# Two reorderings in a fused two-block transformer kernel: state products inside a projection block, and attention quarters of one wide and one narrow query tile

## What is computed

```python
n = rms_norm(h, attn_norm[i])
z = n @ w_in[i]
gq, gk, gv, g_low, g_r, c_q, c_kv, k_r = split_cols(z, IN_SPLITS)
...
def step(state, inp):                      # linear attention, chunks of 64 tokens
    qi, ki, vi, gi = inp
    b = jnp.cumsum(gi, axis=2)
    b_last = b[:, :, -1:, :]
    o_inter = jnp.einsum('bhtk,bhkv->bhtv', qi * jnp.exp(b), state)
    ...
    k_dec = ki * jnp.exp(b_last - b)
    state = state * jnp.exp(b_last[:, :, 0, :, None]) + jnp.einsum('bhsk,bhsv->bhkv', k_dec, vi)
    return state, o_inter + o_intra
...
for blk in range(S // Q_BLOCK):            # latent attention, query tiles of 128 tokens
    qs, qe = blk * Q_BLOCK, (blk + 1) * Q_BLOCK
    qb, kb, vb = q[:, qs:qe], k[:, :qe], v[:, :qe]
    logits = jnp.einsum('bqhd,bkhd->bhqk', qb, kb).astype(jnp.float32) * scale
    ...
    probs = jax.nn.softmax(logits, axis=-1).astype(vb.dtype)
    outs.append(jnp.einsum('bhqk,bkhd->bqhd', probs, vb))
...
h = h + jnp.concatenate([o_g, o_m], axis=-1) @ w_out[i]
```

## Time and profile before

| | |
|---|---|
| median of three runs | 2522.47 us (2522.36 to 2523.17) |
| the profiled execution | 2522.89 us, its span 2521.2 us |
| PE busy | 2457.1 us (97%) |
| DVE busy | 1695.4 us (67%) |
| ACT busy | 1061.8 us (42%) |
| linear attention behind the last projection block | about 226 to 297 us of the span |
| latent attention's 64 units | about 356 to 516 us of the span |

### The profile page before, as it was taken

The page is one execution under the profiler, slowest core; times in us unless marked ns, Lnnn a source line. Parts: engine busy times, 40 slices in busy tenths (PEclk is TensorE's granted clock), DMA queues, the critical chain, the costliest instruction groups (busy, mean ns, idle before and its releaser), DMA issues.

```text
span 2521.2 us, 29558 instructions
## 1 busy us (share of the span) xinstructions
PE 2457.1 (97%) x11406; PEld 1948.0 (77%) x11406; DVE 1695.4 (67%) x2062; ACT 1061.8 (42%) x1500; POOL 125.6 (5%) x215
## 2 busy tenths in 40 slices
PE   8999888999999999999999999999999999999998
PEld 6877755578888888888788777778778888888885
DVE  5237777644877768698873555345578877686888
ACT  5225576634433333333542323343355433334336
POOL 1001000000000010000001000000001000000001
PEclk9998899999999999999999999999999999999999
DMA  5110000033432372600134121124435433616103
GB/s 220 45 42 22 1 1 1 18 133 125 146 114 100 114 278 77 234 1 17 51 108 137 42 67 67 67 100 150 150 126 196 147 114 120 217 51 217 50 1 134
DMA packets 76179, 252.13 MB, mean 100 GB/s; under 512 B 6288, under 2 KB 6320, under 8 KB 76016
## 3 DMA queue, kind: packets, MB, share of 16 engines
q1 hardware_dynamic: 43792, 131.08, 16.0%
q0 software_dynamic: 32256, 119.27, 12.6%
HBM read 186.76 MB, written 62.91 MB: 99 GB/s over the span
## 4 chain that ended last, share of the span: by engine, by line
PE 75%; DVE 10%; issue 3%; ACT 3%; DVEq 0%; ACTq 0%
PE ps L2593 23%; PE ps L2933 20%; PE ps L2971 18%; PE ps L3099 6%; DVE opQ_lo L2037 1%; PE ps L3027 1%; PE ps L3045 1%; DVE opQ_lo L2034 1%; PE ps L2866 1%; DVE spot L2079 1%; DVE ql_raw L2074 1%; PE ps L2896 1%; PE ps L2710 1%; PE ps L2817 1%; PE ps L3036 1%
## 5 line engine op out<-in xcount | busy, mean ns | idle before, releaser
L2971 PE MATMUL ps<-opQ_hi 128*128 128x512 f32 x896 | 350.3, 391 | 2.8 <-DVE opQ_lo L2037 2.8
L2971 PE MATMUL ps<-opQ_hi,opQ_lo 128*128 128x512 f32 x896 | 348.7, 389 | 0.0
L2971 PE MATMUL ps<-opQ_lo,opQ_hi 128*128 128x512 f32 x896 | 348.6, 389 | 0.0
L2593 PE MATMUL ps<-opP_hi,w_hi 128*128 128x512 f32 x640 | 199.6, 393 | 2.3 <-ACT Z L1094 1.1
L2971 PEld LDWEIGHTS ps<-opQ_hi 128*128 128x128 f32 x896 | 168.2, 188 | 42.1 <-DVE opQ_lo L2037 7.2
L2593 PE MATMUL ps<-opP_lo,w_hi 128*128 128x512 f32 x640 | 197.6, 390 | 0.0
L2593 PE MATMUL ps<-opP_hi,w_lo 128*128 128x512 f32 x640 | 197.5, 390 | 0.0
L2971 PEld LDWEIGHTS ps<-opQ_hi,opQ_lo 128*128 128x128 f32 x896 | 168.2, 188 | 35.2
L2971 PEld LDWEIGHTS ps<-opQ_lo,opQ_hi 128*128 128x128 f32 x896 | 168.2, 188 | 34.6 <-issue 0.2
L1214 ACT ACTIVATE opQ_hi<-spot 128x1024 fp32r<-128x1024 f32 x80 | 84.9, 1061 | 235.7 <-PE ps L2971 196.7
L823 ACT ACTIVATE w_hi<-w_stage 128x1024 fp32r<-128x1024 f32 x104 | 109.3, 1051 | 171.8 <-PE ps L2593 148.2
(11 more groups left out here) (425 smaller groups left out, 4809.3 us busy)
## 6 DMA issues: line engine op xcount, KB each, us to landing
w_stage<-in_w_stream SPq DMA_DIRECT2D x104, 512.0 KB, 3.7
h_spill<-T POOLq DMA_DIRECT2D x56, 512.0 KB, 4.9
pair_raw<-in_w_stream SPq DMA_DIRECT2D x26, 1024.0 KB, 5.8
spot<-in_w_stream SPq DMA_DIRECT2D x24, 1024.0 KB, 7.3
spot<-h_spill POOLq DMA_DIRECT2D x24, 1024.0 KB, 9.3
qh_raw<-in_w_stream SPq DMA_DIRECT2D x8, 1024.0 KB, 11.3
ql_raw<-h_spill POOLq DMA_DIRECT2D x8, 1024.0 KB, 8.1
g_spill<-T POOLq DMA_DIRECT2D x16, 512.0 KB, 2.9
```

Source lines behind the costliest of these rows:

```text
L2593: mm = pe.matmul(ps[:, psum + half, :], weight, operand[:, k, half * HALF:(half + 1) * HALF], start=(begin and x == 0 and weight is wh and ...
L2971: mm = pe.matmul(ps[:, down_bank(sc, f) + m, :], weight, operand, start=(g == 0 and kt == 0 and weight is wh and operand is hi), stop=(g = ...
```

## The change

The linear attention's first state products are put between the two halves of the last projection block, the states' folding on DVE is moved ahead with them, and ACT's list is reordered. In the latent attention the quarters become (7, 0), (6, 1), (5, 2), (4, 3), and inside a quarter the wide and the narrow tile alternate. All of the diff is shown but for two short stretches.

```diff
@@ -40,7 +40,7 @@
...
-QBLOCKS = [(pr, qt, par) for pr in range(MH // 2) for qt in range(WIN) for par in range(2)]
+QBLOCKS = [(pr, qt, par) for pr in range(MH // 2) for q in range(4) for par in range(2) for qt in (7 - q, q)]
@@ -310,8 +310,8 @@
             "lexp", "qx", "lk", "lmm", "lcp", "out", "oraw", "sq", "nst", "rn", "sig", "gated", "normed", "fin")}
-        g["dot"], g["wide"] = g["logit"], g["soft"]
-        DOT, WIDE = 2, 1
+        g["dot"], g["wide"], g["upper"] = g["logit"], g["soft"], g["lin"]
+        DOT, WIDE, UPPER = 2, 1, 2
         m = {n: sem("lat_" + n) for n in ("stat", "r", "lat", "sq", "ln")}
@@ -411,7 +411,7 @@
         LEVEL_ORDER = (0, 1, 3, 8, 2, 4, 5, 6, 7, 9, 10, 11)
-        EARLY_LEVELS = 5
+        EARLY_LEVELS = 6
@@ -635,7 +635,7 @@
             pool.memset(QE[0][:, :, :, :, :], 0.0).then_inc(g["zero"], 1)
-            pool.wait_ge(mm_done, B_WOUT)
+            pool.wait_ge(g["upper"], UPPER + 1)
             for pr in range(2):
@@ -960,7 +960,6 @@
             level(8)
-            act.wait_ge(mm_done, B_WOUT)
             level(2)
@@ -988,13 +987,13 @@
             blocks_out(0)
+            level(4)
+            blocks_out(2)
+            diagonal(1, range(WIN)).then_inc(g["diag"], 1)
+            blocks_out(1)
             act.activation(EB[:, :, :], Bc[:, :, :], ACT.Exp, scale=1.0 / 16).then_inc(g["exps"], 1)
...
                 level(n)
-                if n == 4:
-                    blocks_out(2)
-                    diagonal(1, range(WIN)).then_inc(g["diag"], 1)
-                    blocks_out(1)
                 if n == 9:
@@ -1091,8 +1090,9 @@
                 act.wait_ge(mha["pv"], 2 * i + 2)
-                act.activation(Z[:, 8 + i // 2, (i % 2) * HALF:(i % 2 + 1) * HALF], ps[:, 6 + i % 2, :], ACT.Copy)\
-                   .then_inc(mha["o"], 1)
+                tiles = Z[:, 8 + i // 2, :].rearrange("p (x c) -> p x c", c=2 * P)
+                act.activation(tiles[:, 1:3, :] if i % 2 else tiles[:, 0:4:3, :],
+                               ps[:, 6 + i % 2, :].rearrange("p (x c) -> p x c", c=2 * P), ACT.Copy).then_inc(mha["o"], 1)
@@ -1110,12 +1110,12 @@
                     act.wait_ge(mha["pv"], u // 4)
-                act.activation(PT[:, par, 0:n, (qt % 2) * P:(qt % 2 + 1) * P], ps[:, 4, 0:n * P].rearrange("p (k t) -> p k t", t=P),
+                act.activation(PT[:, par, 0:n, (qt // 4) * P:(qt // 4 + 1) * P], ps[:, 4, 0:n * P].rearrange("p (k t) -> p k t", t=P),
                                ACT.Copy).then_inc(mha["ea"], 1)
...
                     act.wait_ge(mha["tb"], upper_groups(u + 1))
-                    act.activation(PT[:, par, 4:4 + n, (qt % 2) * P:(qt % 2 + 1) * P],
+                    act.activation(PT[:, par, 4:4 + n, P:2 * P],
                                    ps[:, 5, 0:n * P].rearrange("p (k t) -> p k t", t=P), ACT.Copy).then_inc(mha["eb"], 1)
@@ -1740,8 +1740,6 @@
             v.tensor_tensor(QK[:, :, :], q_t, k_t, ALU.mult).then_inc(g["qk"], 1)
-            win_step(B_WIN + 15, None, 15, 1, False)
@@ -1749,10 +1747,10 @@
-            def states(pr):
+            def states(pr, steps=range(NCH - 1)):
                 v.wait_ge(g["upd"], pr + 1)
-                for c in range(NCH - 1):
+                for c in steps:
@@ -1776,23 +1774,26 @@
+            v.wait_ge(g["upper"], UPPER + 1)
             exponents(2)
-            factors(2)
-            exponents(4)
             v.wait_ge(g["consts"], 16)
...
                 v.memset(ST8[:, pr, 0, :], 0.0).then_inc(g["states"], 1)
-            states(0)
+            states(0, range(0, 6))
+            win_step(B_WIN + 15, None, 15, 1, False)
+            states(0, range(6, NCH - 1))
+            factors(2)
+            exponents(4)
             for n in range(3, len(GLA_STEPS)):
...
                 if n == 3:
-                    inter_queries(0)
+                    states(1)
                 if GLA_STEPS[n - 1][1] >= 2:
...
                 if n == 4:
-                    states(1)
+                    inter_queries(0)
                 if n == 5:
@@ -2690,8 +2691,6 @@
                     mm.then_inc(g["tr"], 1)
-            w_in(B_WIN + 15, None, 15, 1)
@@ -2768,7 +2767,12 @@
             q_t, k_t = Z[:, 4:6, :], Z[:, 6:8, :]
+            pe.wait_ge(w_lo_done, B_WIN + 16)
+            pe.wait_ge(evac_done, B_WIN + 14)
+            product(2, 1, wcols, opP_hi, opP_lo, (4, 5, 6, 7), lambda k: O_WIN + k + 1, True, end=False).then_inc(g["upper"], 1)
             pe.wait_ge(g["trc"], WIN + 4)
+            updates(0)
+            product(2, 1, wcols, opP_hi, opP_lo, (0, 1, 2, 3), lambda k: O_WIN + k + 1, True, begin=False).then_inc(mm_done, 1)
             pe.wait_ge(g["qk"], QK_MADE + 1)
@@ -2778,13 +2782,12 @@
             block_scores(0)
-            updates(0)
             pe.wait_ge(evac_done, B_WOUT)
             block_scores(1)
+            pe.wait_ge(g["states"], 2 + 15)
+            updates(1)
             block_scores(2)
             level_scores(3)
-            pe.wait_ge(g["states"], 2 + 15)
-            updates(1)
             level_scores(4)
@@ -2888,13 +2891,18 @@
                     pe.wait_ge(mha["o"], i // 2 - 1)
-                last = 2 * quarter + 1
+                last, c = 7 - quarter, quarter % 2
                 for kt in range(last + 1):
-                    c = P if kt == last else 0
                     for par in range(2):
                         h = 2 * pr + par
-                        mm = pe.matmul(ps[64 * par:64 * par + 64, 6 + quarter // 2, (quarter % 2) * 256 + c:(quarter % 2 + 1) * 256],
-                                       VA[:, kt, h * 64:(h + 1) * 64], PT[:, par, kt, c:256], start=(kt == 0), stop=(kt == last))
+                        out = ps[64 * par:64 * par + 64, 6 + quarter // 2, :].rearrange("p (x t) -> p x t", t=P)
+                        both = out[:, c:4 - c:3 - 2 * c, :]
+                        if kt <= quarter:
+                            mm = pe.matmul(both, VA[:, kt, h * 64:(h + 1) * 64], PT[:, par, kt, :].rearrange("p (x t) -> p x t", t=P),
+                                           start=(kt == 0), stop=False)
+                        else:
+                            mm = pe.matmul(out[:, 3 - c, :], VA[:, kt, h * 64:(h + 1) * 64], PT[:, par, kt, P:2 * P],
+                                           start=False, stop=(kt == last))
                 mm.then_inc(mha["pv"], 1)
```

## The result

| | before | after |
|---|---|---|
| median of four runs | 2522.41 us (2521.97 to 2523.17) | 2539.25 us (2538.24 to 2540.53) |
| the profiled execution | 2522.89 us, span 2521.2 | 2540.53 us, span 2538.9 |
| ratio to before | | 1.0066 [1.0054, 1.0077] |

What follows compares the result with a forecast made beforehand. Waits on DVE's state-step chains were taken to bound the linear attention, and PE nearly the latent attention. 2522.9 - 4.8 (linear attention) + 16.6 (latent attention) = 2534.7 us, range 2526 to 2546.

Steps and rivals of the forecast that it cites:

- State part, -4.8: Linear attention: first product of queries and states starts near 250.7 to 252.5, saving 4.8 us, bounds 3 and 9.
- Rival D: Linear attention: moving the state products saves nothing, because reordered ACT ends as late as DVE did; 2539 us, chance 0.09.
- sign of being right: Linear attention: first product of queries and states near 251, with ACT's `EB` as its releaser through DVE.
- Start, +7.5: Latent attention: first values 17.5 us after the first scores instead of 10.0, so 7.5 us slower.
- Pairs, +11.4: Latent attention, three pairs of heads: 41.7 us each, 127.1 in all with 2 us extra, against 115.7; 11.4 us slower.
- inside the series: Latent attention: wide scores, transposes, copies and next wide exponential run serially, 4.76 us at eight key tiles, 3.06 at five.
- Values: Latent attention: value products cost 0.25 us per 128-column tile, 0.456 per wide one; 8.6 us a pair against 8.3.
- Change of pair, 1.9 a pair: Latent attention: DVE takes the wide maximum before normalising the narrow unit, so PE's transposes wait 1.9 us a pair.
- End, -2.3: Latent attention after the last pair's first values: 31.2 us instead of 33.5, so 2.3 us saved.
- Rival A, the clock,: Latent attention: some 5 us at half clock at every change of pair, costing 2 to 3 us each; 2544 us, chance 0.18.
- Rival B: Latent attention: balanced quarters leave PE's own work, about 34 us a pair, as the bound; 2500 us, chance 0.09.
- C: Latent attention: the series overlaps better than counted and loses only 5 us; no change, 2523 us, chance 0.05.

Runs made afterwards that it cites:

- e2: Kernel before with only the change's new quarters in the latent attention, linear attention as before: 2542.75 us, ratio 1.0084.
- e3: Changed kernel with a quarter's units ordered wide, wide, narrow, narrow instead of alternating: 2517.5 us, ratio 0.9979.
- e7: Kernel before with only the linear attention's part of the change, plus ACT's exponential `EB` ahead of the second diagonal: 2527.34 us, ratio 1.0003.
- e11: Kernel before with only the linear attention's part of the change, run a second time: 2519.49 us, ratio 0.9987.
- e1: Kernel before with only the linear attention's part of the change, first run: 2519.39 us, ratio 0.9992.
- e8: Changed kernel with DVE's normalisation of the narrow unit ahead of the wide unit's maximum at each change of pair: 2542.94 us, ratio 1.0075.
- e9: Kernel before with only the unit order inside its old quarters changed (0 1 0 1, 2 3 2 3, 4 5 5 4, 6 7 7 6): 2517.11 us, ratio 0.9979.

## Why the prediction was right, and where its sizes were off

The direction, both signs and the main mechanism held; the profiled execution came 5.8 us above the forecast. Some of its terms came out only because two errors cancelled.

- **State part, -4.8, measured -5.1.** Each instant of the chain can be laid beside its forecast once the 1.2 us lost near 129 us are taken off: `EB` ready at 249.2 (forecast 249.3), `QX` at 250.5 (250.6), the first product at 250.8 (250.7 to 252.5, and 251.2 by the 4.8 taken). The products in the block took 1.98 (1.9). Rival D falls. One thing the prediction left out came out by luck: PE's scores of level 4, at half clock (3.68 us), end just there too, 0.4 us behind `QX`. So the first product was held by ACT's block output through PE, and not by `EB` through DVE, as the prediction's sign of being right had it.
- **Start, +7.5, measured +7.1** (17.1 behind the first scores, forecast 17.5), in part by luck. The first scores, taken at half clock, ran at full clock, and the next wide ones came 4.7 us behind them (forecast 3.6 + 2.8 = 6.4). The step behind those, partly at half clock, took 6.3 us where 4.76 was taken. In e2, where both ran at half clock, the start is 19.8 us.
- **Pairs, +11.4, measured +13.2.** That the order of the units is what costs is shown by the experiments on it. Of what makes it costly, the prediction named both parts, the narrow neighbour and the values ahead of the wide transposes, "inside the series"; the run with the narrow tile first puts about two thirds on the second. A step of seven key tiles took 4.4 us without the values, and the forecast's scale between 3.06 and 4.76 gives 4.2. The last two pairs, 42.5 and 41.8, lie 0.2 below and 0.1 above the forecast with its 2 us spread over two pairs. The first is 1.9 over it: 3.4 us of it, at 399 us behind PE's wait of 2.11 us, ran at half clock, half of which is loss.
- **Values.** A quarter takes 2.1 us in each of the four of a pair (369.52 to 371.64 the first), together 8.4 (forecast 8.6; before 8.4 as well). The first quarter at length:

```profile
369.52 0.65 PE L2901 MATMUL ps<-PT,VA 128*64 128x256 f32 x4
370.01 1.70 PE L2904 MATMUL ps<-PT,VA 128*64 128x128 f32 x28
371.64 0.66 PE L2879 MATMUL ps<-ident,Pb 128*128 128x128 f32 x4
```

  Seven tiles of 128 columns in 1.63 us (370.01 to 371.64) are 0.233 each; the forecast took 0.25. By the rule of the Trainium skill's page "TensorE: Matmul & The Clock Gate", section on the back-to-back issue gap, they would be 0.32, an estimate of four records of about 81 ns; the trace does not agree. Its records come every 58 ns with an operand of 64 columns loaded, and every 124 ns with one of 128 in the row at 278.43 of the earlier trace rows, both at full clock.
- **Change of pair, 1.9 a pair: the attribution failed.** The wait is there (2.11, 1.42 and 1.33 us), but taking its cause away moved nothing. The step "DVE takes the maximum of the wide one before it normalises the narrow one, and PE's transposes wait" names a wait that only hides behind the next link. The total of a pair was right with a wrong item in it.
- **End, -2.3, measured -0.5: mis-sized.** It left the clock out: in e2, whose end ran at full clock, it is 31.0 us, where 31.2 was forecast. In the change the last values, 16 records, started at half clock (3.68 us for 16 records of 256 columns where four take 0.65 at full clock), and the output projection's first products with them, which is the 1.9 us behind the stretch:

```profile
526.25 3.68 PE L2901 MATMUL ps<-PT,VA 128*64 128x256 f32 x16 [0.69 <-ACT PT L1113]
...
531.44 1.19 PE L2594 MATMUL ps<-opP_hi,w_hi 128*128 128x512 f32 x2 [1.08 <-ACT Z L1094]
```

  The same values in e2:

```profile
535.20 1.95 PE L2899 MATMUL ps<-PT,VA 128*64 128x256 f32 x16 [0.69 <-ACT PT L1114]
```

- **Rival A, the clock,** came true in a small part: 3.4 us at half clock in the first pair and 10.2 us from 525 to 535, some 5.6 us of loss (1.7 in the pair, 2.0 in the end and 1.9 behind it) in place of the 9 that it added. The other two pairs were granted 1.00, with waits at the change of 1.42 and 1.33 us. By the Trainium skill's page "TensorE: Matmul & The Clock Gate", section on HAM oscillation, short bursts between waits for data each start slow; carried over to this kernel, as the prediction did, that makes every change of pair a slow start. The trace agrees for one in three, and for the end.
- **Rival B** was nearly right that 34 us a pair is PE's own work (34.3 to 35.9 in the third pair of the kernels with the new quarters), and wrong on both of its conditions: balance brings nothing (the order wide, wide, narrow, narrow is within 0.2% of before), and its remedy, the exponential first, costs some 8 us. **C** falls.

## What to carry to other kernels

In a pipeline of three engines with lists in fixed order and two buffers, what counts is not how much work a quarter holds but what stands beside each link of a unit's chain. A neighbour as large as the unit covers the other engines' time; where the neighbour is small, other work (here the values) does it if it stands behind the transposes that another engine waits for, and adds to the chain if it stands ahead of them. Write the chain of one step out (scores, transposes, copies, exponential, scores) and see which of its links have another unit's work beside them; that gave the pair's length within 5% from rows of the kernel before. Compare with a stretch that ran at full clock in both traces, as the third pair did here. Before an instruction is moved ahead in one list, ask what stands behind it there: in the run with the exponential first, ACT's exponential waited for DVE, with the copies that PE needed behind it.

## What the runs showed of the hardware that was not expected

The stretch at half clock that begins near 242 us, in the waits of the linear attention, is not of one length in kernels with the state part. Most have it for 27 to 31 us; the profiles of e3 and e7 have it for 58.0 and 61.4 us. Windows of the state part run again:

```profile
242.40:273.10 30.70, 22.67 (x246) 22.20 (x248) 25.57 (x41) 14.32 (x30) 0.00 (x0) 0.50 0.00 1
273.10:303.70 30.60, 29.57 (x270) 21.99 (x268) 21.96 (x45) 21.71 (x25) 0.00 (x0) 1.00 0.00 1
```

And of the kernel with `EB` moved ahead:

```profile
241.80:272.70 30.90, 20.89 (x236) 20.64 (x237) 24.11 (x39) 13.58 (x30) 0.00 (x0) 0.50 0.00 1
272.70:303.30 30.60, 30.60 (x220) 27.22 (x220) 19.29 (x36) 11.81 (x12) 0.00 (x0) 0.50 0.00 1
```

In the second window of each PE is busy almost throughout, once at full and once at half clock. From the first product of queries and states to the first scores it is 100.4 us in the one and 114.5 in the other; e3, whose linear attention has the instructions of e11, has 114.7. So it is no property of the instructions. Single executions at 2536 to 2540 us stand among others at 2512 to 2530 in e1, e3 and e7, with a mean granted clock of 0.979 to 0.981 where the others of e1 have 0.988 to 0.990; none of the 65 of the kernel before that ran beside the experiments is over 2528.7. The spread does not come with every set of executions: it was expected again of e11, and the eleven there lie between 2517.4 and 2521.6. Near 129 us, ahead of everything changed, the half clock lasts 0, 3.4 or 6.8 us in kernels with the same instructions there, which moves all that follows by up to 4.1 us (the turn of the decayed keys comes from 211.1 to 215.15). The start of the latent attention, with the same instructions in the change, e2 and e8, has 3.4 us at half clock in the first and some 13 and 11 in the others; the first values come 17.1, 19.8 and 19.5 us behind the first scores.

Two of these differences bear on why the state part's 5.1 us of the trace are about 3 in the medians. In the trace of e11 1.5 us of them are lost at the turn (215.15 against 213.66). And the 42.31 us of before are those of one execution: e9, with the same linear attention, has 41.03. Only the profiled executions have a trace, so what each of them takes of the medians is not shown. What makes the clock fall back at one time and not at another stays open.
